# A hybrid encoder step on one core: tile-boundary steps set apart, norms in three parts, conv state as rows, an earlier value output and a joint key decode

## The chip, the cores and the metric

One Trainium2 chip, one core. The metric is the device time of one execution in microseconds (us); less is better. A time is the median of several runs of the same program.

## What is computed

One layer of a streaming encoder in float32, D_MODEL = 1024, for 512 frames of a new stream and 64 frames of a running one, 576 tokens that share all weights:

```python
h = rms_norm(x, norm1_gain) * (1 + scale1) + shift1      # scale, shift, gate: silu(c) @ w_ada + b_ada
q, k, v, cb, cc, cx, ga, gb = split(h @ w_in)
y_att  = band_softmax_attend(rms_norm(q), rms_norm(k), v) @ w_o_att      # 8 heads x 64
y_conv = (cb * causal_short_conv(cc * cx)) @ w_o_conv                    # width 3
x = x + gate1 * ((sigmoid(ga) * y_att + sigmoid(gb) * y_conv) @ w_o)
h2 = rms_norm(x, norm2_gain) * (1 + scale2) + shift2
q = (h2 @ w_pq)                                 # 8 heads x 2 sides x 128
s1, s2 = scores of both sides against 128 sub keys; v1, i1 = top_k(s1, 16); v2, i2 = top_k(s2, 16)
top_s, pos = top_k(v1[:, None] + v2[None, :], 16); idx = i1[pos // 16] * 128 + i2[pos % 16]
x = x + gate2 * sum_k softmax(top_s)[k] * gelu(expert_u[idx[k]] . h2) * expert_v[idx[k]]
```

The outputs are x of both streams, the new keys and values, and the last two inputs of the convolution of each stream (2 x 512 numbers each, `o_conv_p` and `o_conv_s`). Every token fetches 8 x 16 = 128 rows of `expert_uv` (1024 numbers of u and 1024 of v, 8 KB a row): 604 MB in all.

## The kernel before, in words

The tokens form two groups: A has 256 (group 0), B has 320 (group 1: 256 of the first stream and the 64 of the second). Each group passes the same list of **ticks** (`ticks`): `norm` (the first norm), `z` (the results of the input projection, each in two half pieces), `at` (attention, one tick a head and block of queries), `kn` (keys turned to rows), `mg` (merge), `wo` (output projection), `norm` again, and `rt` (scores of the sub keys and the choice of the top 16, a head at a time). The ada ticks, which make shift, scale and gate, go among those of A.

Behind the choice come the **fetches**. Of 18 tiles with 32 tokens each (`TILES`), every tile has 32 steps called `gather`; step n fetches 128 rows of 8 KB (1 MB) by one indirect DMA from GpSimd into a slot of a ring, one slot is 8 KB a partition. For each fetched slot VectorE makes the dot product with h2 (`dot`, L1518), ScalarE the gelu and a 128x32 matrix of weights (`spread`, L1104 to L1111), and TensorE adds the weighted v rows into PSUM (`fold`, L852), four slots at a time; that frees the slots. At a tile's end come single steps: `keep_sum` (ScalarE copies the sum, L1118), `join` (TensorE L862), `scale` (VectorE L1527), `residual` (TensorE L871), `add` (VectorE L1534), `store` (DMA out), and for the tile to come `natural` (TensorE L832) and `keep_natural` (ScalarE L1088). They stand at fixed steps j of the next tile, and before the change each producer and its consumer stand at the same j.

`order()` writes one list that all engines follow. Group A's ticks come first, with the first 24 ticks of B among them (two norm ticks of B right behind A's norm, then z pieces among A's attention). A's heads of `rt` are decoded one by one, and each released head (`place`: TensorE spreads indices and weights over the partitions, L821, and VectorE copies them, L1504 and L1507) gives four fetches. From fetch 28 on, B's remaining ticks are dealt out over fetches 28 to 236, and they end at fetch 234. From then on only fetches are left, and the choices for the later tiles (`pick`), which VectorE makes ahead in paced steps. Weights come in 1 MB blocks by SyncE (L475) into the same ring: 11 slots while A is worked on, later 3 for weights and 8 for fetches, and from fetch 240 (`EARLY`) all 11 for fetches.

`norm` (L555 on TensorE, L914 on ScalarE, L1197 on VectorE) is two ticks: ScalarE squares the eight tiles of x into two buffers of `tmp` by turns, each of which TensorE must have read before it is filled again; TensorE sums over partitions with a matrix of ones (L563); VectorE makes mean and reciprocal (L1202, L1205), ScalarE the root, VectorE the eight products (L1210); then scale and shift on both engines (L936, L1219).

`pick_head` (from L1363) decodes a head on VectorE; at its end (L1416 to L1421) it looks up the indices of the two sides one after the other, three operations of 256 elements a side.

The order between producer and consumer of a tile's boundary, as one of them reads it:

```python
if j == 4 and g >= 1:
    scale(g - 1)
if j == 8 and g >= 1:
    add(g - 1)
```

## Time and profile before

| | |
|---|---|
| median of 3 runs | 2057.67 us (2056.53 to 2062.09) |
| the profiled execution's own time | 2057.14 us |
| its span | 2055.0 us |
| TensorE busy | 1672.3 us, 81% |
| VectorE busy | 1221.6 us, 59% |
| ScalarE busy | 724.2 us, 35% |
| GpSimd busy | 607.4 us, 30% |
| DMA | 718.23 MB, mean 350 GB/s |
| first fetch issued | 387.5 us from the start |

Busy time is what an engine spends in its own instructions; TensorE's overlaps with itself where matmuls are pipelined. The span runs from the first instruction to the last; 2.1 us of the execution's time lie outside it. The DMA share is the mean busy share of the 16 DMA engines; where it is at 1.0 the queues always had work, and the GB/s beside it tell how much came through. A stretch in which the share falls is one in which no fetch was outstanding, because no slot was free or no index was known.

### The profile page before, as it was taken

Reading aid. Unit: us, or ns where it says so; the run is one execution under the profiler, and the core shown is the slowest. Engines: PE = TensorE matmul, PEld = TensorE weight load, DVE = VectorE, ACT = ScalarE, POOL = GpSimd, SP = SyncE. Lnnn points to the kernel's source line nnn. Section 1 sums busy time; section 2 is a strip of 40 time slices with the busy share of each in tenths; the row PEclk is TensorE's granted clock in tenths of the full one; section 3 lists DMA queues with packets and bytes.
Section 4 is the critical chain, followed back from the end, with each engine's and each line's share of the span. In section 5 each row is a group of like instructions: output and inputs, shape, how many; then the busy total and the mean of one; then the engine's idle time right before and its main releaser. Section 6 shows DMA issues by size and latency. Waiting matters only on the chain.

```text
span 2055.0 us, 22374 instructions
## 1 busy us (share of the span) xinstructions
PE 1672.3 (81%) x7436; PEld 787.0 (38%) x7436; DVE 1221.6 (59%) x3212; ACT 724.2 (35%) x2230; POOL 607.4 (30%) x584
## 2 busy tenths in 40 slices
PE   6999998987878779989788867777777777777776
PEld 3775786853434335444344422121121121111221
DVE  3325212797887764545577667777776566655554
ACT  3115201344355623322433243333333333343332
POOL 0000000134331333333233244434443333434431
PEclk8999999998986889999899999999999999999999
DMA  9457520599995998999998999999999999999995
GB/s 399 180 181 273 201 103 21 213 368 369 396 389 207 356 404 348 421 420 422 392 366 302 265 422 422 421 421 422 421 421 421 422 421 421 421 421 422 421 422 242
DMA packets 102467, 718.23 MB, mean 350 GB/s; under 512 B 13584, under 2 KB 13584, under 8 KB 15568
## 3 DMA queue, kind: packets, MB, share of 16 engines
q0 software_dynamic: 82944, 604.02, 72.5%
q1 hardware_dynamic: 18544, 110.43, 14.0%
q10 hardware_dynamic: 864, 2.36, 0.3%
q8 instruction: 59, 0.97, 0.2%
q14 instruction: 56, 0.46, 0.1%
HBM read 712.04 MB, written 4.73 MB: 349 GB/s over the span
## 4 chain that ended last, share of the span: by engine, by line
DMA 42%; PE 31%; DVE 14%; issue 6%; ACT 4%; POOL 2%; SPq 0%; DVEq 0%; POOLq 0%; ACTq 0%
DMA ring<-in_expert_uv_dram,uidx 41%; PE ps L852 7%; PE ps L594 6%; DVE ring L1518 5%; PE ps L713 5%; POOL ring L463 2%; PE ps L719 2%; PE ps L734 2%; PE ps L772 2%; PE ps L590 1%; DMA ring<-in_wpack_dram 1%; PE ps L563 1%; DMA o_v_s<-kv 1%; ACT wsel L1106 1%; ACT wdiag L1111 1%
## 5 line engine op out<-in xcount | busy, mean ns | idle before, releaser
L852 PE MATMUL ps<-ring,wdiag 128*32 128x512 f32 x2304 | 844.9, 638 | 251.6 <-ACT wdiag L1111 231.8
L463 POOL DMA_INDIRECT ring<-in_expert_uv_dram,uidx x576 | 606.1, 1052 | 1363.9 <-PE ps L852 892.9
L1518 DVE CUSTOM_DVE_ANT_0 ring<-ring,mA 128x1024 f32<-128x1024 f32 x576 | 699.0, 1223 | 452.4 <-DMA ring<-in_expert_uv_dram,uidx 447.2
L852 PEld LDWEIGHTS ps<-ring,wdiag 128*32 128x32 f32 x2304 | 173.3, 114 | 854.4 <-ACT wdiag L1111 519.6
L1104 ACT ACTIVATE gel<-act_in 128x1 f32<-128x1 f32 x576 | 116.7, 203 | 856.4 <-DVE act_in L1518 841.2
L1111 ACT ACTIVATE wdiag<-repeat,wsel 128x32 f32<-128x32 f32 x576 | 185.1, 321 | 18.8
L1106 ACT ACTIVATE wsel<-gel,gsel 128x1 f32<-128x1 f32 x576 | 169.6, 295 | 18.7
L594 PE MATMUL ps<-hB,ring 128*128 128x320 f32 x320 | 94.0, 443 | 1.0 <-ACT convB L969 1.0
L772 PE MATMUL ps<-hB,ring 128*128 128x320 f32 x256 | 77.8, 458 | 8.2 <-issue 8.2
L594 PE MATMUL ps<-hA,ring 128*128 128x256 f32 x320 | 72.5, 387 | 4.2 <-DVE qB L1235 4.2
L713 PE MATMUL ps<-hB,ring 128*128 128x320 f32 x256 | 75.3, 448 | 0.0
L594 PEld LDWEIGHTS ps<-hB,ring 128*128 128x128 f32 x320 | 59.3, 193 | 32.4 <-issue 11.6
L594 PEld LDWEIGHTS ps<-hA,ring 128*128 128x128 f32 x320 | 61.5, 194 | 15.0 <-issue 6.4
L772 PE MATMUL ps<-hA,ring 128*128 128x256 f32 x256 | 58.8, 389 | 7.1 <-DVE hA L1219 7.1
L772 PEld LDWEIGHTS ps<-hB,ring 128*128 128x128 f32 x256 | 49.6, 200 | 38.7 <-issue 22.4
L713 PEld LDWEIGHTS ps<-hB,ring 128*128 128x128 f32 x256 | 48.5, 195 | 32.3 <-issue 15.2
L713 PE MATMUL ps<-hA,ring 128*128 128x256 f32 x256 | 56.6, 379 | 0.0
L772 PEld LDWEIGHTS ps<-hA,ring 128*128 128x128 f32 x256 | 49.6, 196 | 14.3 <-issue 7.5
L713 PEld LDWEIGHTS ps<-hA,ring 128*128 128x128 f32 x256 | 48.6, 190 | 6.6
L1518 DVE DVE_READ_ACCUMULATOR2_ANT act_in<- 128x1 f32 x576 | 47.4, 82 | 0.0
L1342 DVE SCALAR_TENSOR_TENSOR mA<-qB,ps 128x256 f32<-128x256 f32 x8 | 3.4, 421 | 70.0 <-PE ps L719 70.0
L641 PE MATMUL ps<-ident,xB 128*128 128x128 f32 (+1 forms) x96 | 20.6, 318 | 29.0 <-ACT xB L1002 13.2
(238 smaller groups left out, 1626.1 us busy)
## 6 DMA issues: line engine op xcount, KB each, us to landing
ring<-in_wpack_dram SPq DMA_DIRECT2D x96, 1024.0 KB, 5.6
ring<-in_expert_uv_dram,uidx POOLq DMA_INDIRECT x576
xB<-in_x_b_dram SPq DMA_DIRECT2D x2, 1280.0 KB, 19.6
o_y_p<-mA ACTq DMA_DIRECT2D x16, 128.0 KB
xA<-in_x_a_dram SPq DMA_DIRECT2D x1, 1024.0 KB, 5.3
bias<-in_bias_dram SPq DMA_DIRECT2D x1, 1024.0 KB, 32.0
o_v_p<-kv SPq DMA_DIRECT2D x4, 256.0 KB, 10.1
o_k_p<-xB SPq DMA_DIRECT2D x4, 256.0 KB, 10.8
```

Of the source, the lines that this page charges most:

```text
L463: nc.gpsimd.indirect_dma_start(out=ring[:, slot, :], out_offset=None, in_=ins["expert_uv"], in_offset=bass.IndirectOffsetOnAxis(ap=uidx[:, ...
L594: mm = nc.tensor.matmul(ps[:, bank, 0:n], w[:, t, c:c + P], h[g][:, t, :], start=(t == 0), stop=(t == KD - 1))
L641: mm = nc.tensor.transpose(ps[0:kw, bank, at:at + w], att_sc[0:w, u % 3, at:at + kw], ident[0:w, 0:w])
L713: mm = nc.tensor.matmul(ps[:, bank, 0:n], w[:, res, t, :], h[g][:, t, :], start=(t == 0), stop=(t == KD - 1))
L719: mm = nc.tensor.matmul(ps[:, bank, 0:n], w[:, d % 2, res - 2, t, :], src[:, t, :], start=(t == 0), stop=(t == 3))
L734: mm = nc.tensor.matmul(ps[:, BK[g][d % 2], 0:n], w[:, d % 2, t, :], mT[g][:, t, :], start=(t == 0), stop=(t == KD - 1))
L772: mm = nc.tensor.matmul(ps[:, BK[g][m], 0:n], w[:, m, t, :], h[g][:, t, :], start=(t == 0), stop=(t == KD - 1))
L852: mm = nc.tensor.matmul(pY[c * GT:(c + 1) * GT, half, :], wdiag[:, n % NDIAG, :], ring[:, ROW[n][0], D + half * 512:D + (half + 1) * 512], ...
L1104: nc.scalar.activation(gel[:, j:j + 1], act_in[:, g % 2, j:j + 1], ACT.Gelu_apprx_tanh).then_inc(s["gelu"], 1)
L1106: nc.scalar.activation(wsel[:, j:j + 1], gel[:, j:j + 1], ACT.Identity, scale=gsel[:, p % 2, a, j:j + 1]).then_inc(s["weight"], 1)
L1111: nc.scalar.activation(wdiag[:, n % NDIAG, :], repeat[:, :], ACT.Identity, scale=wsel[:, j:j + 1]).then_inc(s["diag"], 1)
L1518: nc.vector.tensor_tensor_reduce(r, r, h2n[:, g % 2, :], 1.0, 0.0, ALU.mult, ALU.add, act_in[:, g % 2, j:j + 1]).then_inc(s["dot"], 1)
```

## The change

- `AHEAD` is 15 and not 12: `place` of a later group of tokens comes three fetches earlier on TensorE, and VectorE's copy, now its own entry `keep`, `KEPT` = 3 fetches behind it. `EARLY` becomes 237, and B's ticks are dealt out over fetches 28 to 233, ending at 231.
- The steps of a tile's boundary are set apart: sum kept at j = 1 of the next tile (before: 31 of its own), gate rows 1 and kept 4 (1 and 1), join 4 and scale 7 (4 and 4), residual 11 and add 14 (8 and 8), store 17 (12), natural 20 and kept 23 (16 and 16); for the first tile 25 and 27.
- `norm` is three ticks. The squares go into `h`, eight tiles of their own, so ScalarE waits for no matmul; TensorE's sum is in the second tick. Four of A's eight ada ticks stand ahead of that sum. B's first norm no longer stands ahead of A's projection, but in three places of it (`NORM_AT`). B's second norm has pauses between its parts (ticks in which nothing is issued, while fetches go on).
- The conv state is transposed on TensorE, copied by ScalarE, and written as 8 rows of 128 numbers (512 B) a stream, two DMAs; before, four DMAs wrote 512 single numbers each.
- The values of B go out (`values_out(1)`) ahead of weight block ("z", 1, 8), not behind the fourth load after the first merge block.
- `pick_head` looks up both sides in one operation of 512 elements, three instead of six. A head is then four paced steps and not five (32 and 16 for 40 and 20).

```diff
-AHEAD = 12
+AHEAD = 15
+KEPT = 3
 EARLY = GT * FIRST[2] - AHEAD - 4
...
     out.append(("norm", 0, 0))
     if g == 0:
-        out += [("ada", 0, t) for t in range(KD)]
+        out += [("ada", 0, t) for t in range(KD // 2)]
     out.append(("norm", 0, 1))
+    if g == 0:
+        out += [("ada", 0, t) for t in range(KD // 2, KD)]
+    out.append(("norm", 0, 2))
...
+    if g == 1:
+        out.append(("state", 0, 0))
...
-    out += [("norm", 1, 0), ("norm", 1, 1)]
+    gap = [("pause", 0, 0)] * g
+    out += [("norm", 1, 0)] + gap + [("norm", 1, 1)] + gap + [("norm", 1, 2)] + 2 * gap
...
-WITH_A = 2 + 2 * (8 + len(TOKENS[1]))
+WITH_A = 3 + 2 * (8 + len(TOKENS[1]))
+NORM_AT = [("z", 6, 1), ("z", 9, 1), ("z", 11, 1)]
...
-        n = 2 if (kind, x, y) == ("norm", 0, 1) or (kind, x) == ("at", 0) else 1 if kind == "at" else 0
+        n = 2 if (kind, x) == ("at", 0) else 1 if kind == "at" or (kind, x, y) in NORM_AT else 0
...
+        if n - KEPT in PLACE_AT[1:]:
+            out.append(("keep", PLACE_AT.index(n - KEPT)))
...
+                    if i == PLACE[("z", 1, 8)]:
+                        values_out(1)
                     if i == PLACE[("m1", 1, 0)] + 4:
-                        values_out(1)
                         keys_out(1)
...
-                    for w in range(2):
-                        sp.wait_ge(s["zd1"], ZD[1][-1])
-                        sp.dma_start(outs[o][0, 0, w].rearrange("(c p) -> p c", p=P),
-                                     cst[:, g, :, w], allow_slow_non_contiguous=True).then_inc(s["conv_out"], 16)
+                    sp.wait_ge(s["state_row"], 1)
+                    sp.dma_start(outs[o][0, 0].rearrange("w (c p) -> (w c) p", p=P),
+                                 state[8 * g:8 * g + 8, :]).then_inc(s["conv_out"], 16)
...
                     for t in range(KD):
                         pe.wait_ge(s[f"sq{g}"], m * KD + t + 1)
-                        nc.tensor.matmul(ps[:, BK[g][0], 0:n], ones[:, :], tmp[g][:, t % 2, :], start=(t == 0),
-                                         stop=(t == KD - 1)).then_inc(s[f"sq_used{g}"], 1)
+                        mm = nc.tensor.matmul(ps[:, BK[g][0], 0:n], ones[:, :].to_broadcast([P, P]), h[g][:, t, :],
+                                              start=(t == 0), stop=(t == KD - 1))
+                    mm.then_inc(s[f"sq_used{g}"], 1)
...
+                def conv_state():
+                    pe.wait_ge(s["kn1"], len(TOKENS[1]))
+                    nc.tensor.transpose(ps[0:16, PT[1][0], 0:P], cst[:, :, :, :].rearrange("p g w c -> p (g w c)"),
+                                        ident[:, :]).then_inc(s["state_ps"], 1)
...
-                    if j == 8 and g:
+                    if j == 11 and g:
                         residual(g - 1)
-                    if j == GT // 2 and g + 1 < NG and g >= 0:
+                    if j == (20 if g else 25) and g + 1 < NG and g >= 0:
                         natural(g + 1)
...
-                            if t >= 2:
-                                act.wait_ge(s[f"sq_used{g}"], m * KD + t - 1)
-                            nc.scalar.square(t_[:, t % 2, :], xT[g][:, t, :]).then_inc(s[f"sq{g}"], 1)
+                            nc.scalar.square(h[g][:, t, :], xT[g][:, t, :]).then_inc(s[f"sq{g}"], 1)
...
-                    if j == GT - 1 and g >= 0:
-                        keep_sum(g)
+                    if j == 1 and g >= 1:
+                        keep_sum(g - 1)
...
-                    if j == GT // 2 and g + 1 < NG and g >= 0:
+                    if j == (23 if g else 27) and g + 1 < NG and g >= 0:
                         keep_natural(g + 1)
...
-                    e4 = cleft.rearrange("p (k a) -> p k a", a=TOPK)
-                    for side in range(2):
-                        cd.did(nc.vector.tensor_tensor(e4, bc(posf[:, side, :], 2, TOPK), bc(iota16[:, :], 1, TOPK),
-                                                       ALU.is_equal))
-                        settle()
-                        cd.did(nc.vector.tensor_tensor(e4, e4, bc(idxf[:, side, :], 1, TOPK), ALU.mult))
-                        settle()
-                        cd.did(nc.vector.tensor_reduce(rows[:, side, hd, :], e4, AX_X, ALU.add))
-                        settle()
-                        if side == 0:
-                            yield
+                    four = [P, 2, TOPK, TOPK]
+                    cd.did(nc.vector.tensor_tensor(hot, posf[:, :, :].unsqueeze(3).to_broadcast(four),
+                                                   iota16[:, :].unsqueeze(1).unsqueeze(1).to_broadcast(four), ALU.is_equal))
+                    settle()
+                    cd.did(nc.vector.tensor_tensor(hot, hot, idxf[:, :, :].unsqueeze(2).to_broadcast(four), ALU.mult))
+                    settle()
+                    cd.did(nc.vector.tensor_reduce(rows[:, :, hd, :], hot, AX_X, ALU.add))
+                    settle()
...
-                    if j == 4 and g >= 1:
+                    if j == 7 and g >= 1:
                         scale(g - 1)
-                    if j == 8 and g >= 1:
+                    if j == 14 and g >= 1:
                         add(g - 1)
```

Line numbers of the changed kernel stand 17 to 29 higher than before: L580 there is L563 here, L612 is L594, L877 is L852, L887 is L862, L896 is L871.

**TensorE at the start.** `ones` is the matrix of the norm's sum, `hA,ring` are results of A's projection, `convB` holds silu(c). Before:

```order
L563 MATMUL ps<-qB,ones 128x256 x8
L546 MATMUL ps<-ring,convB 32x512 x32
L552 MATMUL ps<-ident,left 128x128 x4
L563 MATMUL ps<-tB,ones 128x320 x8
L594 MATMUL ps<-hA,ring 128x256 x16
L601 MATMUL ps<-qB,blk 128x256
```

And now, with the place to which B's sum has gone:

```order
L563 MATMUL ps<-ring,convB 32x512 x16
L580 MATMUL ps<-hA,ones 128x256 x8
L563 MATMUL ps<-ring,convB 32x512 x16
L569 MATMUL ps<-ident,left 128x128 x4
L612 MATMUL ps<-hA,ring 128x256 x16
...
L608 MATMUL ps<-ring,hA 128x256 x8
L580 MATMUL ps<-hB,ones 128x320 x8
L608 MATMUL ps<-ring,hA 128x256 x16
L612 MATMUL ps<-hA,ring 128x256 x96
```

B's sum (128x320) stood ahead of A's first result and now stands among A's value results.

**TensorE in B's attention, at a tile's boundary.** `ring,wdiag` are folds, `kv,qB` scores, `mA,repeat` is the join and `ident,xA` the residual. Before:

```order
L852 MATMUL ps<-ring,wdiag 32x512 x8
L871 MATMUL ps<-ident,xA 32x128 x8
L624 MATMUL ps<-kv,qB 128x512
L641 MATMUL ps<-ident,xB 128x128 x4
L657 MATMUL ps<-kv,xB 128x64 x4
```

And now:

```order
L877 MATMUL ps<-ring,wdiag 32x512 x8
L896 MATMUL ps<-ident,xA 32x128 x8
L642 MATMUL ps<-qB 64x128
L642 MATMUL ps<-kv,qB 64x64
L659 MATMUL ps<-ident,xB 128x128 x4
```

The residual still stands right behind a fold, one fold later in the tile. What differs is VectorE.

**VectorE at the same boundary**, the end of it. `ISA ring,act_in` is the dot of one fetch, the last row is `add`. Before:

```order
L1308 TENSOR_REDUCE stat<-xB 128x1
L1518 ISA ring,act_in<-ring,mA 128x1024
L1518 ISA act_in 128x1
L1518 ISA ring,act_in<-ring,mA 128x1024
L1518 ISA act_in 128x1
L1534 TENSOR_TENSOR mA<-mA,ps 32x1024
```

And now:

```order
L1337 TENSOR_REDUCE stat<-xB 64x1
L1349 RECIPROCAL ssum<-ssum 128x8
L1354 TENSOR_TENSOR xB<-ps,ssum 128x512
L1544 ISA ring,act_in<-ring,mA 128x1024
L1544 ISA act_in 128x1
L1560 TENSOR_TENSOR mA<-mA,ps 32x1024
```

Before, `add` was reached at the same fetch as the residual that it needs; now three fetches of dots and three attention ticks stand between the two.

## Rows read from the trace of the kernel before

**Rows 1.** The page: span, and busy time of each engine.

```profile
span 2055.0 us, 22374 instructions
PE 1672.3 (81%) x7436; PEld 787.0 (38%) x7436; DVE 1221.6 (59%) x3212; ACT 724.2 (35%) x2230; POOL 607.4 (30%) x584
```

**Rows 2.** The page: the chain that ended last, share by engine.

```profile
DMA 42%; PE 31%; DVE 14%; issue 6%; ACT 4%; POOL 2%; SPq 0%; DVEq 0%; POOLq 0%; ACTq 0%
```

**Rows 3.** Windows: stretch, length, busy PE PEld DVE ACT POOL, PEclk, DMA share, GB/s.

```profile
388.00:500.00 112.00, 88.71 (x668) 58.35 (x667) 92.02 (x360) 51.91 (x144) 43.88 (x36) 0.89 0.91 365
500.00:580.00 80.00, 72.69 (x361) 39.46 (x360) 66.27 (x221) 24.47 (x84) 27.56 (x27) 0.96 1.00 405
...
620.00:670.00 50.00, 38.79 (x173) 21.02 (x174) 35.39 (x93) 27.94 (x64) 10.86 (x12) 0.72 0.52 198
670.00:740.00 70.00, 55.56 (x319) 26.57 (x320) 54.42 (x175) 42.55 (x126) 27.75 (x25) 0.88 0.93 374
...
760.00:790.00 30.00, 22.85 (x158) 12.02 (x159) 15.71 (x32) 11.60 (x33) 6.19 (x5) 0.81 0.69 269
790.00:1000.00 210.00, 197.69 (x878) 101.56 (x877) 102.71 (x179) 64.45 (x223) 76.12 (x72) 0.98 1.01 421
1000.00:1050.00 50.00, 34.80 (x143) 18.55 (x142) 32.35 (x88) 22.27 (x62) 11.77 (x13) 0.86 0.86 341
1050.00:1120.00 70.00, 61.22 (x319) 34.25 (x318) 53.13 (x182) 24.57 (x86) 22.04 (x20) 0.95 0.88 352
1120.00:1180.00 60.00, 48.28 (x178) 23.42 (x177) 43.79 (x155) 16.08 (x55) 15.87 (x16) 0.94 1.00 261
...
1240.00:2040.00 800.00, 610.37 (x2112) 148.92 (x2110) 511.71 (x1188) 282.80 (x977) 316.38 (x309) 1.00 1.00 418
```

**Rows 4.** Timeline, TensorE at the start: start, us, line, operation, idle before and releaser.

```profile
33.69 7.02 PE L563 MATMUL ps<-tB,ones 128*128 128x320 f32 x16 [3.47 <-ACT tB L926]
...
40.55 7.07 PE L594 MATMUL ps<-hA,ring 128*128 128x256 f32 x32
...
50.42 5.38 PE L594 MATMUL ps<-hA,ring 128*128 128x256 f32 x16 [1.12 <-DVE qB L1235]
```

**Rows 5.** Timeline: sixteen passes of 320 columns for B, back to back.

```profile
138.23 4.57 PE L594 MATMUL ps<-hB,ring 128*128 128x320 f32 x16
```

**Rows 6.** VectorE's groups by shape: count, busy us, mean ns, idle before.

```profile
L1416 DVE TENSOR_TENSOR left<-posf,iota 128x256 f32<-128x256 f32 x72 | 30.5, 423 | 1.8
L1421 DVE TENSOR_REDUCE rows<-left 128x16 f32<-128x256 f32 x72 | 30.2, 420 | 2.5
...
L1325 DVE TENSOR_TENSOR xB<-ps,ssum 128x512 f32<-128x512 f32 x4 | 2.8, 692 | 1.9 <-PE ps L657 1.8
```

**Rows 7.** Waits, 400 to 500 us: who waited for whom, us, times, longest.

```profile
POOL ring L463 <- DVE gsel L1507: 46.0, 5, 11.8
```

**Rows 8.** Timeline, 618 to 672 us, the boundary of tile 2.

```profile
626.11 1.22 DVE L1527 TENSOR_TENSOR mA<-ps,mA 32x1024 f32<-32x1024 f32 x1 [3.00 <-PE ps L862]
...
647.44 0.94 POOL L463 DMA_INDIRECT ring<-in_expert_uv_dram,uidx  x1 [18.54 <-PE ps L852]
...
649.67 1.21 DVE L1534 TENSOR_TENSOR mA<-mA,ps 32x1024 f32<-32x1024 f32 x1 [7.93 <-PE ps L871]
```

**Rows 9.** Timeline, 740 to 792 us, VectorE's first merge product of B.

```profile
763.45 0.49 DVE L1342 SCALAR_TENSOR_TENSOR kv<-tB,ps 128x320 f32<-128x320 f32 x1 [12.56 <-DMA o_v_s<-kv]
```

**Rows 10.** ScalarE's copies of values (L961): durations in ns, first and last start.

```profile
L961 ACT COPY kv<-ps x10: 354/372/373, 87.2 to 437.4; 128x256 f32<-128x256 f32 x8, 64x256 f32<-64x256 f32 x2
```

**Rows 11.** Timeline, 1000 to 1048 us, GpSimd behind B's second norm.

```profile
1007.38 6.57 PE L563 MATMUL ps<-tB,ones 128*128 128x320 f32 x16 [6.46 <-ACT tB L926]
...
1016.06 0.93 POOL L463 DMA_INDIRECT ring<-in_expert_uv_dram,uidx  x1 [15.81 <-PE ps L852]
```

**Rows 12.** The DMA queues, 1120 to 1180 us.

```profile
DMA packets 4216, 15.65 MB, mean 261 GB/s; under 512 B 2308, under 2 KB 2308, under 8 KB 2308
...
q1 hardware_dynamic: 2072, 0.01, 1.9%
```

69 lines of the change are left out of this document (42 added, 27 removed).

## The prediction

> **What bounds the kernel now.** The page comes first: TensorE is busy for 81% of the span, VectorE for 59% [rows 1]. Neither share says what sets the end, so the chain is read next: 42% of it is DMA and 31% TensorE [rows 2]. The windows then tell where each applies [rows 3]. From 1240 to 2040 us the DMA share is 1.00 at 418 GB/s: the fetches are the bound, and nothing in this change moves fewer bytes there. Before 388 us no fetch runs, and TensorE is the bound. Between 388 and 1240 us it changes. Where the column reads 421 GB/s (790 to 1000 us) DMA is the bound; where it reads less, fetches were held up. I price each such stretch as length x (1 - GB/s / 421), the DMA time lost: 14.9 us in 388 to 500, 3.0 in 500 to 580, 26.5 in 620 to 670, 7.8 in 670 to 740, 10.8 in 760 to 790, 9.5 in 1000 to 1050, 11.5 in 1050 to 1120, 22.8 in 1120 to 1180, all from [rows 3]. That is 106.8 us, the most that better order behind the first fetch can give back. Since the last fetches run in an unbroken queue, each microsecond won here or ahead of the first fetch should arrive at the end.
>
> **The change, part by part.**
>
> **B's first norm leaves the head of A's projection.** TensorE spends 7.02 us on B's sum at 33.69 us, waiting for squares; A's first two results run to 47.6, and the third starts at 50.42 [rows 4], since VectorE and ScalarE were busy with B's norm. A's own inputs were ready when B's sum began. Without B's sum the two results (7.07 us) end at 33.7 + 7.1 = 40.8; the third followed them by 50.42 - 47.6 = 2.8 us, of which some 1 to 2 us is mean and bank release that stays, so it starts near 42. Gain 8.4 us. Back comes B's sum, sixteen passes of 320 columns that cost 4.57 us unhindered [rows 5], in a stretch that TensorE bounds, and ScalarE's eight squares in the query and key results: 4 us of work against some 3 us that it idles per result, so 1 to 2 us. Net 8.4 - 4.6 - 1.5 = **2.3 us**. Bounds: 8.4 (the sum falls into a wait) and -2 (the squares delay two results). Moving four ada ticks ahead of A's sum costs nothing: those matmuls wait for their weight blocks anyway. A's second norm keeps its length, since TensorE's sum is the longer part of it.
>
> **Both sides in one look-up.** Six operations of 256 elements at 0.42 us [rows 6] plus about 0.04 us between each make 2.75 us a head. A 512-element operation took 0.69 us [rows 6]; three with the same gaps make 2.19. So 0.56 us less for each of 28 heads. It counts where VectorE is the bound: in 388 to 500 us it is busy for 92.0 of 112 us [rows 3], and GpSimd waited 46.0 us in five waits for its copy of the indices [rows 7]. Seven heads lie on that path: 7 x 0.56 = **4 us**. Bounds: 0 and the stretch's 14.9. The Trainium skill (VectorE: DVE Perf Modes, section "The TRN2 errata") gives a table entry of 58 cycles plus one per element at 0.96 GHz. By that a 512-element operation would be an estimated 0.59 us and a 256-element one 0.33, a gain of 0.2 us a head and 1.4 us here; the same section says that the entry is too low, and [rows 6] say so too, so the rows' value stands.
>
> **The boundary set apart.** In B's attention VectorE is close to the bound (54.4 of 70 us in 670 to 740, [rows 3]). At the boundary of tile 2 it stood still 3.00 us for the join and 7.93 us for the residual [rows 8], at a point where TensorE waited for weights whose dots stood behind that wait. The fetch after it was held for 18.54 us [rows 8]. With three fetches between producer and consumer both waits go. I take their 10.9 us, **11 us**. Bounds: 0 (the next wait, exponentials for the transposes, takes their place) and the 26.5 of the stretch. Other boundaries lie in DMA-bound stretches and give nothing. `keep`, the later stores and the earlier `place` stand in slack: VectorE's copy stays at the same fetch as before.
>
> **Values out sooner.** VectorE's first merge product of B waited 12.56 us for `o_v_s` [rows 9], because it overwrites the values; folds and fetches queued behind it. The last values are copied at 437 us [rows 10], so the wait goes whole. The stretch lost 10.8 us of DMA: **10 us**. The same bytes go out earlier in a stretch at 0.91 DMA share, at less than 2 us. SyncE's later weight load waits for nothing that isn't done. Bounds 7 and 12.
>
> **B's second norm in three parts.** GpSimd stood for 15.81 us behind it, TensorE's sum took 6.57 us with 6.46 of waiting [rows 11], and the stretch lost 9.5 us. The squares now need no matmul in between, the sum is 4.6 us in one piece, and pauses let folds run between the parts: **6 us**. Bounds 0 and 9.5. In 1050 to 1120 us (11.5 lost) three cheaper heads give 1.7 and the boundary of tile 6 about 2: **4 us**, bounds 0 and 11.5.
>
> **Conv state as rows.** From 1120 to 1180 us the DMA share is 1.00, yet 261 GB/s came through [rows 3]. In it lie 2308 packets under 512 B, nearly all of q1, whose own time is 1.9% [rows 12]. So the single numbers cost little themselves and the fetches beside them ran slow: 22.8 us lost. The Trainium skill (DMA: Bandwidth & Descriptors, section "Why small descriptors are slow (HBM only)") puts the penalty at about 3 cycles and 32 bytes of descriptor a packet; for some 130 packets an engine that is an estimated fraction of a microsecond, and by it the rows would win nothing here. The trace shows the slow fetches at just these packets, so I side with [rows 3, 12]; the page's case is the last rival. The 16 rows of 512 B are too few to see. But 22.8 can't all come back, because other engines stand close behind: TensorE is busy for 48.3 of those 60 us [rows 3]. At least 48.3 us stay, so at most 11.7 of the 60 are won in that stretch: **11 us**. Bounds 4 and 22.8 (if work that is late there is made up behind it). Transpose, copy and their waits cost TensorE and ScalarE under 1 us.
>
> **What the change adds.** B's ticks end three fetches earlier, with five pauses and ticks more: each tick has 5% fewer fetches beside it. In a stretch that DMA bounds this only shifts bytes; in one that B's work bounds, fetches that it covered run later alone, at 2.5 us each (800 us hold some 318 of them, [rows 3]). And 790 to 1000 us has TensorE at 197.7 of 210 us, 94%: 5% more ticks a fetch take it to the edge. I charge **4 us**, bounds 0 and 10.
>
> Sum: 2.3 + 4 + 11 + 10 + 6 + 4 + 11 - 4 = 44.3 us. The profiled execution took 2057.1, the median 2057.7: **2013 us**.
>
> **Rivals.** *The engines step in for the DMA.* VectorE and TensorE run at 75 to 90% in every held-up stretch of [rows 3], with waits on each other; when one wait goes the next comes. Then only waits that have one plain cause go: values 10, decoding 4, conv at its low bound 4, front 1: 19 us, 2039. For it: the many short waits; against it: the waits of [rows 8] are single and long. *Deep recovery.* If slots of slack let late work catch up, the conv's 22.8, the boundary's 26.5 and the norm's 9.5 return almost whole: 44.3 + 11.8 + 13 + 3.5 = 72.6, so 1985. For it: stretches at 421 GB/s still have TensorE at 94%, so such density is reached. *Slower: TensorE becomes the bound of B's whole part.* From fetch 28 to 231 it would hold every fetch; the three fetches that fall behind its end cost 7.5 us, B's sum inside A's projection 4.6 without its gain, and if the waits of [rows 8, 9] reappear as waits for TensorE nothing is won but 4 of the look-up: 2057 + 8 = 2065. It decides when the DMA share in 790 to 1000 us falls below about 0.97. *The conv writes aren't the cause* of the slow 60 us, whose packets own 1.9% of the time [rows 12]: then the 11 us are missing, 2024, inside the main case, with 0.08 of its chance. The Trainium skill's rule above would give this.
>
> **How the numbers follow.** A measurement here tells about 0.3% (6 us) from no change. Main case (1997 to 2030) 0.62, engines step in (2030 to 2048) 0.17, deep recovery (1975 to 1997) 0.13, slower 0.04, no difference 0.04. The range 1984 to 2042 leaves out about half of the deep case, a third of the second and the last two, in all under 0.2. Faster by over 0.3%: 0.62 + 0.17 + 0.13 = 0.92; same 0.04; slower 0.04.
>
> **What would show it.** Right: first fetch issued near 385 us; third result of A near 42 us; no wait of VectorE for `o_v_s`, none of several us for join or residual; DMA at 0.9 or more in the whole stretch of B's attention; about 420 GB/s and no slow stretch of single numbers behind B's last weight block; the last part from fetch 256 as long as before. Wrong: a new long wait of GpSimd for folds in 790 to 1000 us, or A's value results held up behind B's sum.

## The result, and the profile after

On one chip the changed kernel took 2036.49 us in the median of four runs (2034.1 to 2043.05), the kernel before 2058.23 of four: ratio 0.989 [0.987, 0.992], 21.7 us less. Forecast were 44.3 less and 2013. The sign is right and the time lies in the range, but half of the gain is missing. The profiled execution is the slowest of the four (2043.05, span 2041.0), so its rows are read against [rows 3] stretch by stretch, and its end is not used as a time.

The page of the changed kernel: span, busy time, and the chain by engine, against [rows 1, 2].

```profile
span 2041.0 us, 22251 instructions
...
PE 1634.1 (80%) x7437; PEld 784.4 (38%) x7437; DVE 1205.5 (59%) x3104; ACT 721.4 (35%) x2231; POOL 628.5 (31%) x584
...
DMA 42%; PE 29%; DVE 14%; issue 8%; ACT 4%; POOL 3%; SPq 0%; another core or an unknown queue 0%; DVEq 0%; POOLq 0%; ACTq 0%
```

Nothing there says where 22 us went. The windows do, in the stretches and columns of [rows 3]:

```profile
388.00:500.00 112.00, 84.58 (x664) 54.02 (x663) 87.94 (x329) 51.91 (x146) 44.20 (x34) 0.88 0.94 372
500.00:580.00 80.00, 70.01 (x340) 36.92 (x338) 62.28 (x199) 23.57 (x82) 27.17 (x23) 0.96 0.98 404
620.00:670.00 50.00, 39.49 (x192) 22.91 (x192) 33.70 (x93) 30.90 (x75) 9.59 (x10) 0.78 0.54 201
670.00:740.00 70.00, 51.86 (x275) 22.94 (x276) 49.31 (x149) 34.58 (x108) 28.04 (x24) 0.77 0.83 332
760.00:790.00 30.00, 25.21 (x185) 14.61 (x185) 15.79 (x28) 9.77 (x33) 9.98 (x10) 1.00 1.01 422
790.00:1000.00 210.00, 187.25 (x848) 98.16 (x846) 102.96 (x178) 67.04 (x224) 75.77 (x68) 0.96 1.01 419
1000.00:1050.00 50.00, 45.90 (x181) 23.17 (x182) 38.33 (x125) 21.64 (x71) 16.41 (x16) 0.93 0.98 389
1050.00:1120.00 70.00, 63.10 (x316) 34.60 (x315) 51.69 (x166) 22.99 (x80) 23.67 (x21) 0.93 0.88 343
1120.00:1180.00 60.00, 42.03 (x148) 19.13 (x147) 41.54 (x150) 16.43 (x55) 16.78 (x16) 0.86 0.73 279
1240.00:2020.00 780.00, 564.70 (x2075) 143.79 (x2075) 493.70 (x1113) 276.54 (x955) 317.79 (x306) 0.95 1.01 421
```

Two stretches are better: 760 to 790 us went from 269 to 422 GB/s, and 1000 to 1050 from 341 to 389. Two are not: B's attention (620 to 670) stands at 201 GB/s where it had 198, and 670 to 740 is worse than before, 332 against 374 (TensorE's granted clock there is 0.77 for 0.88; whether that is a cause or follows from its waits no run tells). In 1120 to 1180 the small writes are gone and 279 GB/s come through where 261 did; only the share fell, from 1.00 to 0.73. The last part runs at the same rate.

The same by fetches (start of VectorE's dot of that fetch, us, from each kernel's trace; the pieces don't depend on where a window's edge lies):

| dot of fetch | before | after | length of the piece, before to after |
|---|---|---|---|
| 0 | 397.1 | 390.0 | |
| 56 | 579.2 | 577.4 | 182.1 to 187.4 |
| 104 | 740.6 | 744.6 | 161.4 to 167.2 |
| 120 | 801.7 | 794.7 | 61.1 to 50.1 |
| 184 | 997.0 | 994.4 | 195.3 to 199.7 |
| 200 | 1053.7 | 1039.4 | 56.7 to 45.0 |
| 232 | 1176.0 | 1174.0 | 122.3 to 134.6 |
| 256 | 1236.7 | 1223.6 | 60.7 to 49.6 |
| 575 | 2041.0 | 2027.0 | 804.3 to 803.4 |

Kernels that are alike up to fetch 56 (the changed one, a_single_conv, a_paced and a_paced_noC) took 182.3 to 187.4 us for the piece from 0 to 56, so a few us there tell nothing.

Three gains stand there: 7 us ahead of the first fetch, 11 at the values (104 to 120), 12 at the second norm (184 to 200). The heads (200 to 256) give 1.2 us back, and the pieces up to 104 give back 11 in this execution (6 in the one of a_single_conv below).

**Front.** The timeline of TensorE, against [rows 4, 5]: A's third result, and B's sum in its new place.

```profile
42.74 3.69 PE L612 MATMUL ps<-hA,ring 128*128 128x256 f32 x16 [0.61 <-DVE qB L1264]
...
79.41 4.47 PE L580 MATMUL ps<-hB,ones 128*128 128x320 f32 x16
```

42.74 is what I forecast (42), and the sum costs its 4.47 us as priced. The first fetch is issued at 380.4 us, for 387.5 before and the 385 of the forecast.

**Boundary of tile 2 in B's attention.** VectorE's `scale` and `add`, with no wait behind the start, where [rows 8] had 3.00 and 7.93 us:

```profile
642.10 1.22 DVE L1553 TENSOR_TENSOR mA<-ps,mA 32x1024 f32<-32x1024 f32 x1
671.70 1.22 DVE L1560 TENSOR_TENSOR mA<-mA,ps 32x1024 f32<-32x1024 f32 x1
```

GpSimd's fetches there are held as long as before all the same (18.54 us in [rows 8]):

```profile
644.57 0.94 POOL L480 DMA_INDIRECT ring<-in_expert_uv_dram,uidx  x1 [18.80 <-PE ps L877]
...
662.92 0.94 POOL L480 DMA_INDIRECT ring<-in_expert_uv_dram,uidx  x1 [13.50 <-PE ps L877]
```

**Values out.** The merge product that waited 12.56 us for `o_v_s` [rows 9] waits 0.21, and not for a DMA:

```profile
768.22 0.49 DVE L1371 SCALAR_TENSOR_TENSOR kv<-tB,ps 128x320 f32<-128x320 f32 x1 [0.21 <-DVE chosen L1470]
```

**B's second norm.** TensorE's sum has no wait in it and GpSimd's longest wait is 7.72 us, against 6.46 and 15.81 in [rows 11]:

```profile
986.31 4.57 PE L580 MATMUL ps<-hB,ones 128*128 128x320 f32 x16
```

```profile
992.99 0.94 POOL L480 DMA_INDIRECT ring<-in_expert_uv_dram,uidx  x1 [7.72 <-PE ps L877]
```

**B's heads.** The key scores of B's first head start at 1023.6 us and the last ones at 1164.2; before at 1037.1 and 1184.6. That is 21 us a head before and 20 now (from head to head 16 to 26 us), though a head's 5.25 fetches need some 13 us of DMA. VectorE in one head of the changed kernel: behind its last dot it idles 5.16 us (in the code the decode waits there for the head's scores), decodes 8.6 us in one piece, and only then comes the next dot.

```profile
1133.56 1.22 DVE L1544 CUSTOM_DVE_ANT_0 ring<-ring,mA 128x1024 f32<-128x1024 f32 x1
...
1139.95 0.29 DVE L1403 MAX8 val<-qB 128x8 f32<-128x128 f32 x1 [5.16 <-issue]
...
1147.87 0.69 DVE L1449 TENSOR_REDUCE rows<-left 128x32 f32<-128x512 f32 x1
1148.59 1.22 DVE L1544 CUSTOM_DVE_ANT_0 ring<-ring,mA 128x1024 f32<-128x1024 f32 x1
```

The waits of 1125 to 1175 us show the circle: GpSimd for folds, TensorE for the diagonals that follow the dots, VectorE's decode at its own start.

```profile
POOL ring L480 <- PE ps L877: 36.2, 5, 10.9
DVE val L1403 <- issue: 16.3, 2, 11.1
...
PEld ps L877 <- ACT wdiag L1139: 12.0, 4, 6.5
PE ps L877 <- ACT wdiag L1139: 9.1, 3, 5.6
```

From this came two theories. **Term by term**: each part is worth its price, and some prices are wrong. **Lockstep**: where decode, dots, folds and scores wait on each other in a circle, a head takes 20 us of the engines whatever the DMA does, and a part that frees DMA there gains nothing.

### The profile page after: what moved, and what is told of

It reads as the page before. It is cut to its first block, busy times and chain, and to the rows that moved or that the text cites. A ratio compares the mean times of both kernels' runs of the same rounds, so it can differ in the third digit from the quotient of the medians.

```text
span 2041.0 us, 22251 instructions
## 1 busy us (share of the span) xinstructions
PE 1634.1 (80%) x7437; PEld 784.4 (38%) x7437; DVE 1205.5 (59%) x3104; ACT 721.4 (35%) x2231; POOL 628.5 (31%) x584
## 4 chain that ended last, share of the span: by engine, by line
DMA 42%; PE 29%; DVE 14%; issue 8%; ACT 4%; POOL 3%; SPq 0%; another core or an unknown queue 0%; DVEq 0%; POOLq 0%; ACTq 0%
DMA ring<-in_expert_uv_dram,uidx 41%; PE ps L877 7%; PE ps L612 6%; DVE ring L1544 6%; PE ps L736 4%; POOL ring L480 3%; PE ps L757 3%; PE ps L742 2%; DMA ring<-in_wpack_dram 1%; PE ps L608 1%; ACT wsel L1134 1%; PE ps L642 1%; PE ps L857 1%; ACT wdiag L1139 1%; DVE left L1447 1%
## 5 line engine op out<-in xcount | busy, mean ns | idle before, releaser
L877 PE MATMUL ps<-ring,wdiag 128*32 128x512 f32 x2304 | 814.1, 673 | 282.4 <-ACT wdiag L1139 206.6
L480 POOL DMA_INDIRECT ring<-in_expert_uv_dram,uidx x576 | 627.2, 1089 | 1328.8 <-PE ps L877 853.3
L877 PEld LDWEIGHTS ps<-ring,wdiag 128*32 128x32 f32 x2304 | 170.6, 118 | 846.1 <-ACT wdiag L1139 455.2
L612 PE MATMUL ps<-hB,ring 128*128 128x320 f32 x320 | 93.1, 440 | 0.7 <-ACT convB L991 0.7
L612 PE MATMUL ps<-hA,ring 128*128 128x256 f32 x320 | 73.5, 391 | 6.8 <-DVE qB L1264 3.7
L612 PEld LDWEIGHTS ps<-hB,ring 128*128 128x128 f32 x320 | 59.0, 191 | 30.1 <-issue 8.9
L612 PEld LDWEIGHTS ps<-hA,ring 128*128 128x128 f32 x320 | 62.1, 196 | 17.9 <-issue 5.9
L736 PEld LDWEIGHTS ps<-hB,ring 128*128 128x128 f32 x256 | 47.7, 191 | 27.9 <-issue 10.0
L887 PE MATMUL ps<-mA,repeat 128*32 128x512 f32 x72 | 39.6, 678 | 3.7 <-ACT mA L1122 2.5
```

The costliest lines, as they stand in the source:

```text
L480: nc.gpsimd.indirect_dma_start(out=ring[:, slot, :], out_offset=None, in_=ins["expert_uv"], in_offset=bass.IndirectOffsetOnAxis(ap=uidx[:, ...
L612: mm = nc.tensor.matmul(ps[:, bank, 0:n], w[:, t, c:c + P], h[g][:, t, :], start=(t == 0), stop=(t == KD - 1))
L736: mm = nc.tensor.matmul(ps[:, bank, 0:n], w[:, res, t, :], h[g][:, t, :], start=(t == 0), stop=(t == KD - 1))
L877: mm = nc.tensor.matmul(pY[c * GT:(c + 1) * GT, half, :], wdiag[:, n % NDIAG, :], ring[:, ROW[n][0], D + half * 512:D + (half + 1) * 512], ...
L887: mm = nc.tensor.matmul(pG[a * GT:(a + 1) * GT, half * 512:(half + 1) * 512], repeat[:, :], prod[:, half * 512:(half + 1) * 512], start=Tr ...
```

## The experiments

All times are medians; the ratio is to the kernel before on the same chip, with its 95% interval.

### Parts alone, on the kernel before

**b_conv**: conv state as rows only (the transpose tick, ScalarE's copy, two DMAs of rows for four of single numbers).

> The kernel before with the conv state as rows alone. Term by term (the prediction's sum): 11 us faster than before, about 2047. Lockstep theory (TensorE and VectorE wait for each other in turns while B's heads are decoded, so a faster DMA is not used there): under 5 us, 2053 to 2058, with GB/s near 420 where the DMA share is 1, but a share well under 1 in the 60 us behind B's last weight block.

Measured: 2066.48 us, ratio 1.0015 [1.0006, 1.0024]. No gain. The window from 1120 to 1180 us, against the one of [rows 3] with 1.00 and 261:

```profile
1120.00:1180.00 60.00, 46.49 (x182) 23.32 (x180) 40.20 (x140) 18.46 (x63) 16.41 (x16) 0.89 0.75 285
```

The share fell by a quarter, the bytes rose by 9%, the time didn't fall. The 11 us of the forecast were never there on this kernel. GpSimd, which issues the fetches, was waiting for folds for half of that stretch (waits of the kernel before, 1110 to 1200 us):

```profile
POOL ring L463 <- PE ps L852: 48.9, 9, 11.2
```

**b_values**: `values_out(1)` ahead of block ("z", 1, 8) only.

> The kernel before with the values of B out sooner alone. Both theories: the 12.6 us wait of VectorE for o_v_s is gone. Term by term: 10 us faster, 2048. Lockstep: 7 to 11 us, since this wait has one plain cause and the stretch behind it is bound by DMA.

Measured: 2054.12 us, 0.9957 [0.9944, 0.997], 8.9 us less. As priced (10, bounds 7 and 12).

**b_steps**: the boundary's steps apart only, for instance

```diff
-                    if j == 4 and g >= 1:
+                    if j == 7 and g >= 1:
                         scale(g - 1)
```

> The kernel before with the boundary's steps set apart alone (norm, place and decoding as before). Term by term: 11 us faster, 2047, because VectorE's waits of 3.0 and 7.9 us for join and residual in B's attention go. Lockstep: within 4 us of before, since the next wait (for scores and exponentials) takes their place.

Measured: 2050.0 us, 0.994 [0.9927, 0.9953], 12.4 us less. Fetches 64 to 80 took 59.2 us in place of 67.3, so here the attention did gain its 8.

**b_norms**: the norms in three parts only, with `NORM_AT`, the split ada ticks and the pauses.

> The kernel before, with the norms alone in three parts (the sum as one matmul row per tile with ones widened on the fly, three steps at places of their own, ada's matmuls split around them, pauses in B's part). Term by term by the trace of the changed kernel: about 5 us at the front (row 0's fetch came 7.1 us earlier with all parts together) and 6 to 9 in B's second norm (rows 184 to 192 took 20.0 us in place of 29.2): 2043 to 2052 where the kernel before has 2058 to 2063 (8 to 16 us less). If the gain behind B's second norm is only moved to the folds behind it (B's heads in lockstep), 2 to 6 us less.

Measured: 2038.53 us, 0.989 [0.9871, 0.9909], 22.8 us less: above both expectations, and as much as the whole change. The first dot comes 6.7 us earlier, fetches 184 to 200 take 47.7 us for 56.7, and fetches 104 to 120 another 5 less.

By their ratios the four parts sum to -22.7 - 8.9 - 12.4 + 3.1 = 41 us less. The changed kernel holds them all and gains 22. So the prices were not the main fault: in the combination something takes 19 us back.

### Parts taken out of the changed kernel

**a_oldsteps**: boundary steps at their old places.

> The changed kernel with the boundary's steps where they were. Term by term: 11 us slower than the changed kernel, 2047. Lockstep: within 4 us of the changed kernel, 2032 to 2040. If the steps set apart do harm in the attention, it is faster than the changed kernel.

Measured: 2046.05 us, 0.9919 [0.9903, 0.9935], against the changed kernel's 0.9894 [0.9869, 0.9919]: about 5 us, at the edge of what is told apart. In the attention nothing is lost (fetches 64 to 80 took 69.2 us, 68.0 with the steps apart); fetches 104 to 120 took 59.7 us for 50.0. There the run has a wait that neither kernel of the pair has: with `keep` three fetches behind `place`, `natural` at its old step 16 stands between the two and TensorE waits there until `keep` has copied out the part of PSUM that both use.

```profile
779.37 3.64 PE L857 MATMUL ps<-ident,hA 128*32 128x128 f32 x64 [12.11 <-DVE gsel L1532]
```

So the 5 us are not the steps' worth in the combination; without this wait the old steps might have cost nothing, which no run shows.

**a_single_conv**: conv state as single numbers.

> The changed kernel with the conv state written as single numbers as before. Term by term (the prediction's 11 us): 2043 to 2050, where the changed kernel has 2036. Lockstep theory: conv rows cost and save nothing, as they did on the kernel before (ratio 1.0015): 2034 to 2039. The window from 1120 to 1180 us would show shorter fetch packets with rows and the same row times.

Measured: 2033.53 us, 0.9863 [0.9843, 0.9884]. The rows gain nothing here either.

**a_two_lookups**: the two sides looked up one after the other, five pieces a head, paces 40, 40 and 20.

> The changed kernel with the two sides of a head looked up one after the other again, six operations of 256 elements in five pieces in place of three of 512 in four, and the decode's pace numbers as before. Term by term (the prediction's 4 us in A's heads): 2039 to 2043 where the changed kernel has 2036. Rival, that the new pace of the decode (32 instead of 40 pieces, each longer) is what takes the moved steps' gain in B's attention away: rows 64 to 80 take 59 us again in place of 67, and the kernel lands at 2028 to 2036.

Measured: 2036.2 us, 0.9877 [0.9854, 0.9899]. No difference from the changed kernel. Neither the 4 us of the forecast nor the rival (fetches 64 to 80 took 66.8 us). The look-up was not tried alone on the kernel before.

### The ticks' spread

**a_ticks_late**:

```diff
-AHEAD = 15
-KEPT = 3
+AHEAD = 12
+KEPT = 0
```

> The changed kernel with the ticks of a group of heads ending where they did (12 fetches ahead of what needs them instead of 15, and no fetches kept back). Term by term (the prediction's minus 4 for the compression): 2030 to 2034 where the changed kernel has 2036. Rival, the lockstep in B's heads sets the time there whatever the phase: 2034 to 2040. Third: the shorter distance between a group's places and its gathers costs a wait of GpSimd's on each, 2040 to 2050.

Measured: 2012.94 us, 0.9758 [0.9737, 0.9779]: 49.9 us less than before, 24 less than the changed kernel by the medians and 28 by the ratios. All three expectations missed. This one edit, priced at 4 us, is the missing half. But it is two edits: places three fetches later (with `EARLY` back at 240), and B's ticks dealt out up to fetch 234, not 231. The next two part them, from the changed kernel and from a_ticks_late.

**a_span**: the ticks alone get their old spread.

```diff
-        while done < len(left) and done * (PLACE_AT[2] - 8 - RUN) < (n + 1 - RUN) * len(left):
+        while done < len(left) and done * (PLACE_AT[2] - 5 - RUN) < (n + 1 - RUN) * len(left):
```

> The changed kernel with its places 15 fetches ahead as it has them, but the ticks of B spread to the fetch at which they ended in a_ticks_late (234 rather than 231). If the ticks' density and phase against the folds are what cost 23 us: 2012 to 2018. If it is the places or the ring's widening: 2032 to 2039. Rows 64 to 80 take 58 us in the first case and 67 in the second.

**a_late_short**: the places alone (`AHEAD` 12, `KEPT` 0, and 11 in place of 8 in the same line).

> The opposite half: places 12 fetches ahead as in a_ticks_late, the ticks of B ending at fetch 231 as in the changed kernel. Density and phase: 2032 to 2040. Places: 2010 to 2018.

Measured: a_span 2017.43 us, 0.9787 [0.9772, 0.9802]; a_late_short 2037.05 us, 0.989 [0.9876, 0.9905]. Both lie where the theory of the ticks had them. It is the ticks' spread; the places' distance costs nothing that shows (a_span is 4.5 us, or 6 by the ratios, above a_ticks_late). The score matmuls of B's attention (shortest, median and longest duration in ns, then first and last start in us), in a_late_short and then in a_ticks_late:

```profile
L642 PE MATMUL ps<-kv,qB x48: 213/520/1217, 576.7 to 694.3; 64*128 64x384 f32 x16, 64*128 64x512 f32 x16, 64*64 64x64 f32 x16
```

```profile
L642 PE MATMUL ps<-kv,qB x48: 216/572/1219, 574.3 to 677.8; 64*128 64x384 f32 x16, 64*128 64x512 f32 x16, 64*64 64x64 f32 x16
```

117.6 us against 103.5, with the same instructions; the heads' last scores come 14.9 us earlier in the second (1142.1 for 1157.0), almost all of it from here. The other piece is plain: behind the last head the fetches run alone, and with ticks up to 234 three fewer are left, 3 x 2.5 = 7.5 us. 14.9 + 7.5 = 22.4, where the medians differ by 24.1 and the ratios by 27.

**a_at_late**: a_late_short with the ticks up to the attention's end at the fetches that a_ticks_late gives them, the rest dealt out up to 231.

```diff
+    first = sum(t[0] in ("z", "at", "kn") for t in left)
+    at, fetch = [], float(RUN)
+    for i in range(len(left)):
+        at.append(fetch)
+        fetch += (PLACE_AT[2] - 8 - RUN) / len(left) if i < first else \
+            (PLACE_AT[2] - 11 - at[first]) / (len(left) - first)
...
-        while done < len(left) and done * (PLACE_AT[2] - 8 - RUN) < (n + 1 - RUN) * len(left):
+        while done < len(left) and at[done] < n + 1:
```

> As a_late_short (2037 us; ticks end at fetch 231), but B's ticks up to the end of its attention at the very fetches that they have in a_ticks_late (2013 us), only the merge, the norm and the heads closer together. If the two pieces of the 23 us are separate: the attention's 14 to 15 us come back and the three fetches' 7.5 us do not: 2019 to 2025, rows 64 to 80 in 58 us, the heads ending at the same fetch 231 as in a_late_short. If denser ticks anywhere cost the whole: 2033 to 2038. If only the attention counts: 2010 to 2016.

Measured: 2018.17 us, 0.9799 [0.9783, 0.9814]. The attention's part alone brings 18.9 us back and leaves 5 (8 by the ratios): two separate pieces, as read, the attention's a little larger, so that the time lies 0.8 us under the 2019 of the first case (fetches 64 to 80 took 60.5 us).

**b_short**: the same shift of the ticks' end (8 to 11) on the kernel before.

> The kernel before with the end of B's ticks alone moved three fetches earlier. If denser ticks cost whatever the phase (1.5 per cent fewer fetches under 153 ticks, with B's stages bound by the engines): 8 to 25 us slower than before. If what counts is the phase of a single tick against a fold, and the changed kernel merely fell badly: anything from 5 faster to 10 slower.

Measured: 2060.93 us, 1.0005 [0.9993, 1.0018]. There it costs nothing. Density as such is therefore not the price of the attention. In the kernel before the scores already took 120.8 us, and with the shift 117.1; kernels with the same attention differ by as much (115.7 in a_paced, 120.4 in the changed kernel), so what makes up for the three fetches isn't shown. What is left is which tick meets which fold and boundary step.

The traces show where they meet badly. The fold of fetches 64 to 67, the first of tile 2, in the changed kernel and then in a_ticks_late:

```profile
614.86 1.94 PE L877 MATMUL ps<-ring,wdiag 128*32 128x512 f32 x12 [0.46 <-ACT mA L1146]
...
621.00 3.56 PE L877 MATMUL ps<-ring,wdiag 128*32 128x512 f32 x4 [4.20 <-ACT wdiag L1139]
```

```profile
613.48 3.06 PE L877 MATMUL ps<-ring,wdiag 128*32 128x512 f32 x16
```

In the changed kernel TensorE folds three slots and waits for the fourth diagonal, which on ScalarE stands behind two exponentials of the attention (its dot starts at 614.75 us, its diagonal at 620.62). In a_ticks_late it stands ahead of them (607.06 and 611.82), and the fold runs in one piece. All eight kernels that spread the attention's ticks as the changed one does have this gap, and from this fold to that of fetches 72 to 75 they take 42.9 to 48.3 us; the five with the old spread have none and take 32.8 to 34.1. That is some 11 of the 15 us. (The kernel before has 41.5 there without the gap, behind the waits of [rows 8], and b_steps 32.8.) No run moves that one tick alone.

### B's heads

**a_paced**: the changed kernel, B's decode given out in its four pieces, one at each of a head's four ticks.

```diff
+                    if g == 1 and hd:
+                        if q == 0:
+                            dve.wait_ge(s["sc_sb1"], len(TOKENS[1]) * hd)
+                            split[:] = [pick_head(2, hd - 1)]
+                        for _ in range(4 if hd == PH else 1):
+                            next(split[0])
+                        return
```

> The changed kernel, with VectorE's decode of B's heads given out in four pieces, one at each of the four key-product steps of a head, where the changed kernel decodes a head whole (about 9 us) at the first of them; folds' diagonals and dots come between the pieces. Theory lockstep (in B's heads VectorE's whole decode holds back the diagonals for TensorE's folds, TensorE in its order then comes late with the next scores, and VectorE idles; some 20 us go to a head whatever the DMA does): the period of B's heads falls from 19.9 toward 17 us, the stage gets 10 to 25 us shorter, and the kernel lands at 2012 to 2028 us where the changed kernel has 2036. Theory DMA (the stage is bound by the fetches' transfers and by the small packets beside them): no gain, 2033 to 2040. A third possibility: the decode's last piece now comes later than before, the next head's transposes wait for it and the stage gets longer, 2040 to 2050.

Measured: 2004.95 us, 0.973 [0.9709, 0.9751], 31 us less than the changed kernel (34 by the ratios) with the same instructions: lockstep's direction, and more than its 2012 to 2028. The key scores of B (durations in ns, first and last start in us), changed kernel and then a_paced, 140.6 us against 112.4:

```profile
L775 PE MATMUL ps<-bias,convB x96: 272/275/377, 1023.6 to 1164.2; 128*128 128x128 f32 x64, 128*64 128x128 f32 x32
```

```profile
L775 PE MATMUL ps<-bias,convB x96: 272/275/377, 1014.3 to 1126.7; 128*128 128x128 f32 x64, 128*64 128x128 f32 x32
```

VectorE there has dots between the pieces:

```profile
1084.15 0.28 DVE L1408 MATCH_REPLACE8 left<-val,qB 128x128 f32<-128x128 f32 x1
1084.34 1.21 DVE L1553 CUSTOM_DVE_ANT_0 ring<-ring,mA 128x1024 f32<-128x1024 f32 x1
...
1086.80 0.41 DVE L1420 TENSOR_TENSOR qB<-val 128x256 f32<-128x256 f32 x1
1087.14 1.21 DVE L1553 CUSTOM_DVE_ANT_0 ring<-ring,mA 128x1024 f32<-128x1024 f32 x1
```

Lockstep is shown: the work is the same, only its order differs.

**a_paced_noC**: a_paced with the conv state as single numbers.

> As a_paced, but with the conv state written as single numbers as before (2048 writes of four bytes in place of rows). Conv state as rows alone gained nothing before (ratio 1.0015). Theory lockstep: the small packets only filled time in which the folds were the bound; once the decode is given out in pieces and the stage leans on the DMA, they cost something: 4 to 15 us above a_paced. If they cost nothing here either (within 3 us of a_paced), then the DMA has room in this stage even with the pieces, and what bounds the heads is still a chain of the engines.

Measured: 2014.69 us, 0.9767 [0.9747, 0.9788], 9.7 above a_paced (7.6 by the ratios, whose intervals overlap by a hair). The place fits: fetches 200 to 232, beside which the single numbers are written, took 116.8 us against 106.5. Once the engines let the DMA be the bound, the rows are worth about what I had forecast. Windows from 1050 to 1120 us, a_paced and then a_paced_noC:

```profile
1050.00:1120.00 70.00, 68.01 (x349) 37.72 (x348) 63.60 (x228) 28.41 (x95) 23.87 (x23) 1.00 0.99 406
```

```profile
1050.00:1120.00 70.00, 64.53 (x337) 36.57 (x332) 57.07 (x204) 23.85 (x82) 24.78 (x23) 0.98 1.02 349
```

**a_paced_two**: a_paced with the two look-ups one after the other.

> The best kernel so far (decode of B's heads in pieces, 2005 us), with the two look-ups one after the other as before, the last two of five pieces given out together. If the joint look-up's 0.4 to 1 us a head counts once the heads are no longer in lockstep: 2006 to 2010. If its saving is off the path that bounds: 2003 to 2007. If the pace rival of a_two_lookups holds (attention 8 us shorter): 1996 to 2002.

Measured: 2010.84 us, 0.9758 [0.9738, 0.9778]: 5.8 us above a_paced, with intervals that overlap. By the fetches the difference stands ahead of fetch 56, where alike kernels differ by 5 us, and only 1.4 us in fetches 200 to 232. So a gain of the joint look-up is possible and not shown, and the last two of its five pieces given out together are a rival.

**a_paced_late**: a_paced with `AHEAD` 12 and `KEPT` 0.

> The best kernel so far with the ticks ending 12 fetches ahead instead of 15. With B's heads bound by the DMA (15.8 us a head), the compression has room to cost nothing there, and what is left of it lies in B's attention: 2000 to 2005. If the late places cost GpSimd waits: 2008 to 2020.

Measured: 1991.53 us, 0.9655 [0.9635, 0.9675], below both expectations. The fastest kernel of the study, 71 us below the kernel before and 45 to 49 below the changed one. By its trace a head now takes 16 us with 5.25 fetches, and the attention's scores 104.0 us.

**a_paced_later**: its ticks spread three fetches further, to 237.

> The best kernel so far (1991.5 us: B's decode in pieces, ticks 12 fetches ahead) with its ticks spread three fetches further, to 237. Density: 5 to 15 us faster again, 1977 to 1987. Phase alone: 1985 to 2005. If the last decode now ends behind the place that needs it (fetch 244): a stop of some 5 to 10 us at row 244, which eats the gain.

Measured: 2001.88 us, 0.9722 [0.9707, 0.9736]: slower. At the dot of fetch 104 it is already 8.6 us behind a_paced_late, 3.2 of it ahead of fetch 56 and the rest in the attention (scores 111.0 us for 104.0), and the heads don't win it back. The fold of fetches 64 to 67 has no gap here, but those of 60 to 63 and 84 to 87 wait for their last diagonal by 3.6 and 4.6 us. The same instructions at fetches further apart take longer, so it isn't the density.

**a_paced_share**: a_paced_late with weights for the distance of ticks, 0.93 for `mg` and `wo`, 1.136 for `rt`.

> The best kernel so far (1991.5 us), with the ticks of B's merge and output projection, where the DMA is the bound, 7 per cent closer together and those of the heads 13.6 per cent further apart, so that six fetches more run under the heads (186 to 234 in place of 192 to 234); the attention's ticks stay. A head takes 16.1 us of the engines and its 5.25 fetches 13.2 us of DMA; with 6 fetches it is 15.1. If the fetches before the heads come at 2.51 us and the heads keep their 16 us: up to 15 us faster, 1976 to 1984. If TensorE (busy 0.90 between 740 and 1000 us) can't do the merge any denser: 1985 to 1993.

Measured: 1993.19 us, 0.9684 [0.967, 0.9698]: a miss. B's first key scores come 14.6 us earlier and the last at the same time (1118.9 us, 1119.4 without): a head now takes 18 us for 16, with six fetches in place of 5.25. The merge could be done denser; the heads didn't keep their 16 us, and the experiment doesn't show why.

## Why the prediction missed half of the gain

44.3 us were forecast and 21.7 came. The step that failed is the term for the denser ticks ("I charge 4 us, bounds 0 and 10"): the runs show 19 to 24 in its place. The 11 us of the conv rows and the 4 of the look-up weren't there either, but the norms gave about as much more than their price.

**B's first norm and the front: under-sized.** 2.3 us were forecast, the first dot came 7.1 earlier. The 8.4 won and 4.6 lost were nearly right (A's query and key results end 9.4 us earlier, behind B's sum 5.1 are left). Wrong was the 1.5 us for ScalarE's squares, which cost nothing (a result takes its 4.74 us with or without them), and A's own second norm, which I said keeps its length, became some 1 us shorter.

**B's second norm: under-sized.** 6 us, by the fetches 9 in b_norms and 12 in the change. The norms together are worth 22.8 us alone, where I had 8.3, or 12.3 with the term for 1050 to 1120.

**Values: right** in mechanism and size, 8.9 for 10.

**Boundary: right alone, wrong in the combination.** The 11 us were 12.4 alone, 8 of them in the attention, where they were looked for. In the change the two waits of [rows 8] are gone and the fetches are held for 18.80 us as before. The sign that I had named, DMA at 0.9 or more through B's attention, isn't there. I had named this as the term's lower bound, "the next wait takes their place", and priced the term as if the order around it stayed. It didn't: the ticks' new spread belongs to the same change, and the wait that took their place is the one for the fourth diagonal.

**Joint look-up: wrong in the combination.** 4 us forecast, none measured. VectorE's busy share of 0.82 in 388 to 500 us was read as the bound of a serial chain; what the chain there is bound by, no run shows.

**Conv rows: the step that failed was "share 1.00 and 261 GB/s, so the DMA sets the time".** The share says that the queues had work, not that anything waited for them. GpSimd waited for folds in that stretch (48.9 us in nine waits), and b_conv moved the share from 1.00 to 0.75 without moving the time. My cap of 11.7 us from TensorE's 48.3 busy us was no bound either: a circle of waits has no engine at 100%. The last rival (conv writes not the cause, 2024) was nearer for the kernel as it is, but its reason was wrong: a_paced_noC shows that the writes do slow the fetches. The Trainium skill (DMA: Bandwidth & Descriptors, section "Why small descriptors are slow (HBM only)") would price them at next to nothing by the estimate in the prediction; where the stage leans on the DMA, the run's 9.7 us decide against that.

**Compression: the term that was mis-sized, and the main fault.** 4 us with bounds 0 and 10; 19 and 24 measured (a_span, a_ticks_late; 22 and 28 by the ratios). The 2.5 us for each fetch that falls behind the ticks is right, 7.5 for three, and stood in the prediction only in the slower rival. The rest, some 15 us, is B's attention falling into a worse meeting with the folds, above all with that of fetches 64 to 67, which no sum over instructions shows. By b_short the same shift cost nothing on the kernel before, so the price belongs to the combination. Without this term the forecast's other parts sum to 48.3 us, and the change without the edit gained 49.9: partly by luck, since 15 us of conv and look-up that weren't there stand against the 10 to 14 that the norms gave beyond their price.

Of the rivals, "engines step in" (2039) gave nearly the measured 2036.5, and its mechanism, one wait taking another's place, is what stands in the heads and at the boundary. Its number is luck all the same: it counts 4 us each for decoding and conv rows, which weren't there, and nothing for the norms, worth 22.8 alone.

Two slips stand in the working. The rival says that VectorE and TensorE run at 75 to 90% in every held-up stretch; [rows 3] have VectorE at 52% in 760 to 790 us and 65% in 1000 to 1050. And deep recovery adds 13 us for the boundary, where 26.5 less the 11 already counted is 15.5, so its time would be 1983 and not 1985. Neither moves the forecast.

**Open.** The wait of the fold of fetches 64 to 67 is read from traces; no run takes it away alone, and some 4 of the 15 us lie elsewhere. TensorE's granted clock over 580 to 740 us is 0.78 in a_late_short and 0.83 in a_ticks_late, and how much of the loss is that no run tells. The part of b_norms' gain between fetches 104 and 120 has no cause shown.

## What to carry to other kernels

A busy DMA queue is no proof that the DMA is waited for: ask what the issuer of the next transfer waits for, and if that is a circle of engines each below 100%, look for the longest block in one engine's order and split it before anything else. A constant that only moves when work is dealt out deserves a sweep of its own before and after every other change, since here it was worth as much as all other parts together and hid half of them, while on the kernel before it was worth nothing. Test parts both alone and taken out: the difference between the sum and the whole is where the next gain lies.

## What the runs showed of the hardware

The 2048 single-number writes do hurt the transfers beside them. In a_paced_noC, with the fetches queued behind each other, the DMAs of 512 numbers (2 KB) each of `o_conv_s` took 42.9 us to land in the median, and the core's 16 DMA engines read as busy at 1.02 while 349 GB/s came through, against 406 at 0.99 with rows of 512 B: 57 GB/s over 70 us, 4 MB, which is 9.5 us at 421 GB/s and fits the 9.7 us measured. The packets of the fetches show it too: those of 8 KB that started in 1120 to 1150 us took 520 ns in the mean in the kernel before, beside the single numbers, and 339 in b_conv, with a median of 309 in both. On that kernel nothing waited for them.

The boundary's steps set apart lower TensorE's clock in the last part, at no cost. ScalarE copies a tile's sum at step 1 of the next tile, so that tile's first fold waits for it (6.45 us here, 1.75 at the same place of the kernel before), and the clock is granted at the lower of its two levels, 1.2 GHz, for 7 to 10 us in each of the ten tiles:

```profile
1311.64 4.41 PE L877 MATMUL ps<-ring,wdiag 128*32 128x512 f32 x14 [6.45 <-ACT mA L1146]
```

```profile
1310.00:1318.00 8.00, 6.36 (x21) 1.75 (x22) 5.51 (x17) 3.84 (x13) 2.16 (x2) 0.57 1.01 421
```

Over 1240 to 2000 us the granted clock is 0.94 to 0.96 in every kernel with the steps apart and 0.98 to 1.00 in the others, with 421 GB/s and the DMA as the bound in the changed kernel and the one before.
